# Attention maxima cut into parts of 512 keys, two shared banks for maxima and rows, and loads issued when the scores end

## The chip, the cores and the metric

The kernel runs on one core of a Trainium2 chip. The metric is the device time of one execution in microseconds; a kernel's time is the median of its runs.

## What is computed

Three layers run over 1024 tokens of width 1024 (the second and the third also see 256 context tokens). The change lies in the attentions of layers two and three:

```python
def gqa_attend(q, k, v):          # 16 query heads, 4 key heads, width 64
    s = jnp.einsum('bqhgd,bkhd->bhgqk', q, k).astype(jnp.float32) * (GQA_HEAD_DIM ** -0.5)
    p = jax.nn.softmax(s, axis=-1).astype(v.dtype)
    return jnp.einsum('bhgqk,bkhd->bqhgd', p, v)

def mla_attend(q_nope, q_rope, k_nope, k_rope, v):   # 16 heads, width 64 + 32
    s = (jnp.einsum('bqhd,bkhd->bhqk', q_nope, k_nope)
         + jnp.einsum('bqhr,bkr->bhqk', q_rope, k_rope)).astype(jnp.float32) * ((MLA_NOPE + MLA_ROPE) ** -0.5)
    p = jax.nn.softmax(s, axis=-1).astype(v.dtype)
    return jnp.einsum('bhqk,bkhd->bqhd', p, v)
```

Both take 1280 keys (256 of them context). In gqa the 256 context queries are attended as well, over the context keys alone.

## The kernel before

Float32 products are made of high and low parts. The class `Attention` (L1779) is used twice: `gqa` (three chunks of queries c: 512, 512 and the 256 context queries) and `mla` (two chunks of 512). A Fori loop runs over 8 pairs of heads; within a pair the steps k are unrolled (`self.steps`), one step being one tile of 128 keys against one chunk of queries: 22 steps a head in gqa (10, 10 and 2), 20 in mla.

In a step TensorE makes the scores (`scores`, L1964: two matmuls in gqa, three in mla, into one of two banks `self.S`), ScalarE takes exp and then the high part (`probs`, L2024), GpSimd, or VectorE in steps 3 and 8 of each ten, the low part (`low`, L2058), and TensorE three matmuls of `values` (L1984) that lag by `LAG` = 3 steps. At the end of a chunk ScalarE makes 1/denominator (`rden`, L2036: Ln, then Exp) and VectorE multiplies by it and by the gate (`final`, L2095), both in the step in which that chunk's last values are made.

The softmax needs the row maxima before the scores. They are made from the high parts of the queries: `maxima` (L1939) makes the scores of 128 queries against all 1280 keys, in three matmuls into the three banks of `PMX`, and one VectorE reduction (L2083) takes their maximum. After the tiles of a chunk `diag` (L2086) spreads the maxima over a diagonal, `bcast` (L1956) turns that into rows with a matmul by ones into the bank `self.BC`, and ScalarE's `row` (L2017) copies the one row that is needed into the query tile, where it enters the score matmul. Which step of a head makes which maxima, for the other chunks or for the next head, stands in the list `plan` (L1826 to L1832), four tiles for a chunk of 512 and two for the context chunk. All engines follow their own instructions in order: in a step, TensorE does the planned tasks, then scores, then the lagging values; VectorE does the reductions and the diagonal, then the low part of the step before, then `final`.

SyncE (`sp`, L1905) waits until all values of a head are made, then loads keys, values and queries of the head after the next into its buffers. The first maxima of a head wait for all of these (`loaded`).

## Time and profile before

| | us |
|---|---|
| median of 3 runs | 3587.86 |
| lowest and highest of them | 3587.32, 3591.61 |
| profiled execution | 3586.85 |
| its span, first to last instruction | 3585.0 |
| TensorE busy in the span | 3351.6 |
| mean granted TensorE clock, as a share | 0.977 |

The gqa stage lies at about 1819 to 2385 us of the span, the mla stage at about 2917 to 3490 us. A timeline row gives start, duration, engine and operation, and in brackets how long the engine had been idle and what ended that. A row of groups gives the busy time and the mean of one instruction, then the idle time ahead of the group.

### The profile page before, as it was taken

Reading aid. Unit: us, or ns where it says so; the run is one execution under the profiler, and the core shown is the slowest. Engines: PE = TensorE matmul, PEld = TensorE weight load, DVE = VectorE, ACT = ScalarE, POOL = GpSimd, SP = SyncE. Lnnn points to the kernel's source line nnn. Section 1 sums busy time; section 2 is a strip of 40 time slices with the busy share of each in tenths; the row PEclk is TensorE's granted clock in tenths of the full one; section 3 lists DMA queues with packets and bytes.
Section 4 is the critical chain, followed back from the end, with each engine's and each line's share of the span. In section 5 each row is a group of like instructions: output and inputs, shape, how many; then the busy total and the mean of one; then the engine's idle time right before and its main releaser. Section 6 shows DMA issues by size and latency. Waiting matters only on the chain.

```text
span 3585.0 us, 47856 instructions
## 1 busy us (share of the span) xinstructions
PE 3351.6 (93%) x14934; PEld 2655.1 (74%) x14934; DVE 2186.5 (61%) x2655; ACT 1793.4 (50%) x3060; POOL 1535.2 (43%) x977
## 2 busy tenths in 40 slices
PE   7999999999999999799889999989888989999999
PEld 5777877778888887587777777767765667777767
DVE  6674877477575757447246666666558865555551
ACT  3343868242010101434158888861465657887870
POOL 3303444434444444510156666656210026666652
PEclk9999999999999999899999999999999989999999
DMA  2134232311212121123433443412254344332311
GB/s 99 53 117 119 75 77 81 119 41 66 75 59 88 55 86 35 58 102 115 124 89 66 102 85 76 103 64 89 97 197 149 118 118 111 65 82 53 76 42 71
DMA packets 196086, 313.52 MB, mean 87 GB/s; under 512 B 100928, under 2 KB 111680, under 8 KB 195968
## 3 DMA queue, kind: packets, MB, share of 16 engines
q1 hardware_dynamic: 195968, 312.01, 29.8%
q8 instruction: 67, 1.10, 0.1%
q14 instruction: 51, 0.42, 0.0%
HBM read 234.02 MB, written 77.92 MB: 87 GB/s over the span
## 4 chain that ended last, share of the span: by engine, by line
PE 68%; DVE 12%; issue 7%; ACT 6%; POOL 3%; DMA 2%; SPq 2%; DVEq 0%; ACTq 0%; POOLq 0%
PE PBX L281 10%; PE PBX L283 10%; PE PBX L282 10%; PE PMX L281 5%; PE PMX L282 5%; PE PMX L283 5%; PE PMX L1952 4%; PE PD L1993 2%; PE PD L1994 2%; PE PD L1995 2%; PE PD L856 2%; DVE gqa_m L2083 1%; PE PBX L1977 1%; PE PBX L1976 1%; PE PBX L1978 1%
## 5 line engine op out<-in xcount | busy, mean ns | idle before, releaser
L216 POOL TENSOR_TENSOR w_hi<-w_stage,zero 128x1024 fp32r<-128x1024 f32 (+2 forms) x123 | 229.1, 1863 | 1263.4 <-PE PBX L283 789.3
L2061 POOL TENSOR_TENSOR gqa_pl<-gqa_pf,gqa_ph 128x512 fp32r<-128x512 f32 (+1 forms) x288 | 370.9, 1305 | 186.3 <-ACT gqa_ph L2034 185.7
L2061 POOL TENSOR_TENSOR mla_pl<-mla_pf,mla_ph 128x512 fp32r<-128x512 f32 x256 | 351.8, 1383 | 206.9 <-ACT mla_ph L2034 202.7
L2083 DVE TENSOR_REDUCE gqa_m<-PMX 128x1 f32<-128x1280 f32 (+1 forms) x158 | 200.9, 1271 | 173.6 <-PE PMX L1952 172.7
L218 POOL TENSOR_TENSOR w_lo<-w_stage,w_hi 128x1024 fp32r<-128x1024 f32 (+2 forms) x123 | 299.9, 2438 | 9.7
L1678 ACT ACTIVATE conv_in<-PBX 128x512 f32<-128x512 f32 x66 | 39.6, 601 | 480.6 <-PE PBX L283 476.6
L2083 DVE TENSOR_REDUCE mla_m<-PMX 128x1 f32<-128x1280 f32 x126 | 187.3, 1487 | 89.5 <-PE PMX L1952 88.9
L2029 ACT ACTIVATE mla_pf<-PBX 128x512 f32<-128x512 f32 x320 | 190.1, 594 | 98.0 <-PE PBX L1978 88.1
L2029 ACT ACTIVATE gqa_pf<-PBX 128x512 f32<-128x512 f32 (+1 forms) x352 | 202.1, 574 | 52.8 <-PE PBX L1981 48.6
L2034 ACT ACTIVATE gqa_ph<-gqa_pf 128x512 fp32r<-128x512 f32 (+1 forms) x352 | 215.6, 612 | 13.8
L281 PE MATMUL PBX<-ffn_hi,w_hi 128*128 128x512 f32 x528 | 207.5, 393 | 8.5 <-DVE ffn_lo L653 8.5
L2034 ACT ACTIVATE mla_ph<-mla_pf 128x512 fp32r<-128x512 f32 x320 | 202.2, 632 | 13.2 <-ACT mla_pf L2029 0.8
L283 PE MATMUL PBX<-ffn_hi,w_lo 128*128 128x512 f32 x528 | 206.2, 391 | 0.0
L282 PE MATMUL PBX<-ffn_lo,w_hi 128*128 128x512 f32 x528 | 206.2, 390 | 0.0
L1705 DVE SCALAR_TENSOR_TENSOR conv_out<-conv_in,VEC,conv_out 128x1024 f32<-128x1024 f32 x88 | 187.0, 2125 | 12.8 <-DVE conv_out L1701 0.6
L281 PE MATMUL PBX<-l_hi,w_hi 128*128 128x512 f32 (+1 forms) x408 | 161.8, 397 | 22.6 <-DVE l_lo L653 17.5
L1701 DVE TENSOR_SCALAR conv_out<-conv_in,VEC 128x1024 f32<-128x1024 f32 x44 | 73.8, 1678 | 137.6 <-ACT conv_in L1678 137.4
L432 DVE SCALAR_TENSOR_TENSOR PMX<-mod_w,cond_s 128x1024 f32<-128x1024 f32 x96 | 151.7, 1581 | 5.7 <-DVE PMX L432 0.8
L1440 POOL TENSOR_TENSOR swa_pl<-swa_pf,swa_ph 128x512 fp32r<-128x512 f32 x64 | 81.2, 1269 | 158.2 <-ACT swa_ph L1384 158.0
L283 PE MATMUL PBX<-l_hi,w_lo 128*128 128x512 f32 (+1 forms) x408 | 148.9, 365 | 0.0
L282 PE MATMUL PBX<-l_lo,w_hi 128*128 128x512 f32 (+1 forms) x408 | 148.5, 364 | 0.0
L281 PE MATMUL PBX<-h_hi,w_hi 128*128 128x512 f32 x336 | 138.5, 412 | 7.8 <-POOL w_lo L1426 5.7
(411 smaller groups left out, 9915.1 us busy)
## 6 DMA issues: line engine op xcount, KB each, us to landing
mod_w<-in_w_mod SPq DMA_DIRECT2D x48, 512.0 KB, 3.5
w_stage<-in_w_up SPq DMA_DIRECT2D x44, 512.0 KB, 3.4
w_stage<-in_w_go SPq DMA_DIRECT2D x24, 512.0 KB, 3.8
gqa_k<-kh_d SPq DMA_DIRECT2D x32, 320.0 KB, 4.9
gqa_q<-qh_d SPq DMA_DIRECT2D x32, 320.0 KB, 7.7
w_stage<-in_w_down SPq DMA_DIRECT2D x24, 384.0 KB, 3.0
qh_d<-heads_qh SPq DMA_DIRECT2D x32, 256.0 KB, 2.0
ql_d<-heads_ql SPq DMA_DIRECT2D x32, 256.0 KB, 2.3
```

The lines of the kernel that those rows point to most:

```text
L216: pool.tensor_tensor(w_hi[s][:, 0:st.cols], w_stage[s][:, 0:st.cols], z, ALU.add).then_inc(w_hi_done, 1)
L218: pool.tensor_tensor(w_lo[s][:, 0:st.cols], w_stage[s][:, 0:st.cols], w_hi[s][:, 0:st.cols].bitcast(F32), ALU.subtract).then_inc(w_split, 1)
L281: pe.matmul(ps, wh, xh, start=first, stop=False)
L282: pe.matmul(ps, wh, xl, start=False, stop=False)
L283: return pe.matmul(ps, wl, xh, start=False, stop=last)
L432: dve.scalar_tensor_tensor(out=PMX[:, C:3 * C], in0=bufs[s], scalar=1.0, in1=conds[j], op0=ALU.mult, op1=ALU.mult, accum_out=MOD[:, bass.d ...
L1705: dve.scalar_tensor_tensor(out=y, in0=CU[s][:, j:j + S], scalar=w(j), in1=y, op0=ALU.mult, op1=ALU.add).then_inc(conv_step, 1)
L1952: mm = pe.matmul(MX[:, s - lo_:e - lo_], self.Q[q][0][0:mr, o:o + P], self.K[q][0][0:mr, s:e], start=True, stop=True)
L2029: act.activation(self.PF[k % 4][:, 0:n], self.S[k % 2][:, 0:n], ACT.Exp, scale=self.scale)\
L2034: act.activation(self.PH[k % 4][:, 0:n], self.PF[k % 4][:, 0:n], ACT.Copy).then_inc(self.hi, 1)
L2061: eng.tensor_tensor(self.PL[k % 4][:, 0:n], self.PF[k % 4][:, 0:n], self.PH[k % 4][:, 0:n].bitcast(F32), ALU.subtract).then_inc(self.lo_dv ...
L2083: dve.tensor_reduce(self.M[g % 2][:, t:t + 1], MX[:, 0:w], AX.X, ALU.max, negate=True)\
```

## The change

- Maxima are made and reduced in parts of 512, 512 and 256 keys, each with a matmul, a wait and a reduction of its own (a unit). Units alternate between two banks, `self.MX`; a unit waits until the reduction before the last has ended. A small extra reduction takes the maximum over the parts (`NEG`) ahead of the diagonal.
- The rows go through the same two banks, as units, and VectorE copies them (`row`), in place of ScalarE. Units and rows are planned anew: a tile takes two steps, part 0 in the first and parts 1 and 2 in the second; in gqa the maxima of chunk 1 lie in steps 0 to 5 and its row in step 7, those of the context in 7 and 8 (row 10), those of the next head in 10 to 17 (row 19), and its chunk 1's first tile in 19 and 20. In mla: 0 to 5 (row 7), 9 to 16 (row 18), 18 and 19.
- The freed banks go to scores (three in gqa, four in mla) and, in gqa, to a third output bank. The ring of probabilities has 6 buffers in gqa and 5 in mla, in place of 4. Values lag by 4 steps, in place of 3; `final` runs 2 steps after that on VectorE and writes through the mix tile.
- The two key tiles of the context chunk become one step of 2 x 256 columns (21 steps a head in gqa).
- Loads: high keys and queries are issued when the last scores of the buffer's head have ended, and have a semaphore of their own that the maxima wait for; low queries and values come later, when the values have ended, for head 1 behind the gate's load.

```diff
-        CR_PV2, CR_SC, CR_B, CR_E, CR_ROW2, CR_R, CR_N, CR_FIN2 = 4, 1, 2, 2, 1, 1, 2, 1
+        CR_SC, CR_N, CR_FIN2 = 1, 3, 1
...
-            LAG = 3
+            LAG = 4
...
+                self.PF = [scope.sb(f"{name}_pf{b}", [P, C]) for b in range(ring)]
+                self.PH = [scope.sb(f"{name}_ph{b}", [P, C], R32) for b in range(ring)]
+                self.PL = [scope.sb(f"{name}_pl{b}", [P, C], R32) for b in range(ring)]
+                self.M = scope.sb(f"{name}_m", [P, 4, 3])
+                self.NEG = scope.sb(f"{name}_neg", [P, 4])
+                self.D = scope.sb(f"{name}_d", [P, 4, P], R32)
...
-                self.S = [PB[0], PB[1]]
-                self.BC = PB[2]
-                self.O = [PD[0], PD[1]]
+                self.S = [PB[0], PB[1], PB[2]] + [PMX[:, 2 * C:3 * C]] * self.mla
+                self.NS, self.NP = len(self.S), len(self.PF)
+                self.O = [PD[0], PD[1], PMX[:, 2 * C:3 * C]][:len(chunks)]
+                self.MX = [PMX[:, 0:C], PMX[:, C:2 * C]]
+
+
+                self.groups = [[(t,) for t in keys[c]] if len(keys[c]) > 2 else [tuple(keys[c])]
+                               for c in range(len(chunks))]
+                self.steps = [(q, c, g, x == 0, x == len(self.groups[c]) - 1) for q in range(2)
+                              for c in range(len(chunks)) for x, g in enumerate(self.groups[c])]
...
+                def tiles(at, first, count, step):
+                    return [(step + 2 * t + min(p, 1), "max", at, first + t, p) for t in range(count) for p in range(3)]
 
                 if self.mla:
-                    plan = [(2 * t, "max", (0, 1), t) for t in range(4)] + [(8, "bcast", (0, 1), 0)]
-                    plan += [(10 + 2 * t, "max", (1, 0), t) for t in range(4)] + [(18, "bcast", (1, 0), 0)]
+                    plan = tiles((0, 1), 1, 3, 0) + [(7, "row", (0, 1), 0, 0)]
+                    plan += tiles((1, 0), 0, 4, 9) + [(18, "row", (1, 0), 0, 0)]
+                    plan += tiles((1, 1), 0, 1, 18)
                 else:
-                    plan = [(2 * t, "max", (0, 1), t) for t in range(4)] + [(8, "bcast", (0, 1), 0)]
-                    plan += [(8 + 2 * t, "max", (0, 2), t) for t in range(2)] + [(12, "bcast", (0, 2), 0)]
-                    plan += [(12 + 2 * t, "max", (1, 0), t) for t in range(4)] + [(21, "bcast", (1, 0), 0)]
+                    plan = tiles((0, 1), 1, 3, 0) + [(7, "row", (0, 1), 0, 0)]
+                    plan += [(7 + t, "max", (0, 2), t, 0) for t in range(2)] + [(10, "row", (0, 2), 0, 0)]
+                    plan += tiles((1, 0), 0, 4, 10) + [(19, "row", (1, 0), 0, 0)]
...
+                parts = [(K[0][0:64, :], kh, self.loaded_max)]
+                parts += [(K[1][0:64, :], kl, self.loaded)] if self.mla else \
+                         [(K[0][64:128, :], kl, self.loaded_max), (K[1][0:64, :], kh, self.loaded)]
+                for to, src, done in parts:
+                    sp.dma_start(to.bitcast(F32), src).then_inc(done[q], 16)
...
+                for lo in ((0,) if self.mla else (0, 64)):
+                    sp.dma_start(self.Q[q][0][lo:lo + r, :].bitcast(F32), qh_d[bass.ds(h * r, r), 0:self.nq])\
+                      .then_inc(self.loaded_max[q], 16)
...
-                    sp.wait_ge(self.pv, i * self.SB + CR_PV2)
-                    self.load_kv(sp, 1, kv_row(i, 1))
+                    sp.wait_ge(self.scores, i * self.SB + CR_SC)
+                    self.load_k(sp, 1, kv_row(i, 1))
                     self.load_q(sp, 1, i * 2 + 1)
+                    sp.wait_ge(self.pv, i * self.SB + self.NP)
 
                     sp.wait_ge(self.fin, i * (2 * self.NC) + CR_FIN2)
                     sp.dma_start(self.G[:, :], gate_d[bass.ds(i, 1), :, 0:self.nq].rearrange("o p n -> (o p) n"))\
                       .then_inc(self.gate_loaded, 16)
+                    self.load_q_lo(sp, 1, i * 2 + 1)
+                    self.load_v(sp, 1, kv_row(i, 1))
                     if not last:
-                        sp.wait_ge(self.pv, i * self.SB + (CR_PV2 + self.SB // 2))
-                        self.load_kv(sp, 0, kv_row(i + 1, 0))
+                        sp.wait_ge(self.scores, i * self.SB + (CR_SC + self.SB // 2))
+                        self.load_k(sp, 0, kv_row(i + 1, 0))
                         self.load_q(sp, 0, i * 2 + 2)
+                        sp.wait_ge(self.pv, i * self.SB + (self.NP + self.SB // 2))
+                        self.load_q_lo(sp, 0, i * 2 + 2)
+                        self.load_v(sp, 0, kv_row(i + 1, 0))
...
-                def maxima(i, q, c, t, tile, first_of_head, head, MX=PMX, free=CR_R):
-                    if first_of_head and q == 1:
+                def maxima(i, q, c, t, part, unit, new_head, head, MX=self.MX):
+                    if new_head and q == 1:
                         pe.wait_ge(self.const[1], self.const_n)
-                    if first_of_head:
-
-                        pe.wait_ge(self.loaded[q], head * self.load_inc + self.load_inc)
+                    if unit >= len(MX):
+
+                        pe.wait_ge(self.red, i * (2 * self.NU) + (unit - len(MX) + 1))
...
-                    lo_, hi_ = kt[0] * P, (kt[-1] + 1) * P
-                    for s in range(lo_, hi_, C):
-                        e = min(s + C, hi_)
-                        mm = pe.matmul(MX[:, s - lo_:e - lo_], self.Q[q][0][0:mr, o:o + P], self.K[q][0][0:mr, s:e],
-                                       start=True, stop=True)
-                    mm.then_inc(self.max, 1)
+                    lo, hi = self.part_keys(c, part)
+                    pe.matmul(MX[unit % len(MX)][:, 0:hi - lo], self.Q[q][0][0:mr, o:o + P], self.K[q][0][0:mr, lo:hi],
+                              start=True, stop=True).then_inc(self.max, 1)
...
+                    pe.wait_ge(self.red, i * (2 * self.NU) + (unit - len(self.MX) + 1))
+                    pe.matmul(self.MX[unit % len(self.MX)][:, 0:n], ones[:, :], self.D[:, 0:n // P, :], start=True, stop=True)\
+                      .then_inc(self.max, 1)
...
+                        pe.wait_ge(self.red, i * (2 * self.NU) + (self.row_unit(q, c) + 1))
+                    if first and c == 0:
+
+                        pe.wait_ge(self.loaded[q], i * self.load_inc + self.load_inc)
+
+                    pe.wait_ge(self.exp, i * SB + (k + 1))
...
+                    for p in range(3):
+                        maxima(0, 0, 0, t, p, 3 * t + p, t == 0 and p == 0, 0, self.MX + self.S)
+                bcast(0, 0, 0, 12)
+                for p in range(3):
+                    maxima(0, 0, 1, 0, p, 13 + p, False, 0)
...
-                    act.activation(dst, self.BC[r:r + 1, 0:n], ACT.Copy).then_inc(self.row_done, 1)
...
+                    dve.tensor_reduce(self.M[:, t, part:part + 1], MX[unit % len(MX)][:, 0:hi - lo], AX.X, ALU.max)                       .then_inc(self.red, 1)
+
+                def diag(i, c, g, unit):
+                    m = self.chunks[c][1] // P
+                    parts = 1 if len(self.keys[c]) == 2 else 3
+                    dve.wait_ge(self.red, i * R + (unit + 1))
+                    dve.tensor_reduce(self.NEG[:, 0:m], self.M[:, 0:m, 0:parts], AX.X, ALU.max, negate=True)\
+                       .then_inc(self.neg, 1)
+                    dve.wait_ge(self.neg, i * (2 * NC) + (g + 1))
+                    dve.tensor_tensor(self.D[:, 0:m, :], ident_f[:, :].unsqueeze(1).to_broadcast([P, m, P]),
+                                      self.NEG[:, 0:m].unsqueeze(2).to_broadcast([P, m, P]), ALU.mult)\
+                       .then_inc(self.diag, 1)
+
+                def row(i, q, c, unit):
+                    o, n = self.chunks[c]
+                    r = self.row
+                    dve.wait_ge(self.max, i * R + (unit + 1))
+                    dve.tensor_copy(self.Q[q][0 if self.mla else 1][r:r + 1, o:o + n], self.MX[unit % 2][r:r + 1, 0:n])\
                        .then_inc(self.red, 1)
...
-                    dve.tensor_tensor(self.T[h, 0:n], self.O[x % 2][0:64, 0:n], self.RD[:, 0:n], ALU.mult)\
+                    m = self.mix[h, bass.ds(i, 1), o:o + n].rearrange("p o n -> p (o n)")
+                    dve.tensor_tensor(m, self.O[c][0:64, 0:n], self.RD[64 * (x % 2):64 * (x % 2) + 64, 0:n], ALU.mult)\
...
+                row(0, 0, 0, 12)
+                for p in range(3):
+                    maxima(0, 1, 0, p, 1, 13 + p)
...
-                self.run(dve, step, lambda i, k: final(i, k) if self.steps[k][4] else None)
+                self.run(dve, step, lambda i, k: final(i, k) if self.steps[k][4] else None, lag=self.LAG + 2)
```

## Rows read from the trace of the kernel before

**Rows 1.** Stretches (us): PE, PEld, DVE, ACT, POOL busy (x count), granted clock, DMA share, GB/s.

```profile
1960.00:2100.00 140.00, 128.36 (x569) 99.87 (x568) 86.38 (x94) 122.13 (x216) 95.63 (x75) 1.00 0.41 84
3060.00:3200.00 140.00, 137.76 (x595) 108.21 (x594) 79.83 (x75) 112.76 (x189) 88.70 (x65) 1.00 0.31 67
```

**Rows 2.** By tile: score matmuls: ns min/median/max, first and last start; shapes.

```profile
L1980 PE MATMUL PBX<-gqa_q,gqa_k x352: 277/395/628, 1828.8 to 2375.7; 128*128 128x512 f32 x160, 128*128 128x256 f32 x16
...
L1976 PE MATMUL PBX<-mla_q,mla_k x320: 391/396/632, 2928.2 to 3481.0; 97*128 97x512 f32 x160
```

**Rows 3.** Timeline, gqa, PE: start us, duration, engine, line, output<-inputs.

```profile
2037.18 0.28 PE L1994 MATMUL PD<-gqa_ph,gqa_v 128*128 128x256 f32 x1
...
2037.30 0.28 PE L1995 MATMUL PD<-gqa_pl,gqa_v 128*128 128x256 f32 x1
...
2042.53 0.39 PE L1980 MATMUL PBX<-gqa_q,gqa_k 128*128 128x512 f32 x1
...
2044.87 0.73 PE L1952 MATMUL PMX<-gqa_k,gqa_q 128*128 128x512 f32 x3
```

**Rows 4.** TensorE waits in 1829:2375 (gqa), then 2928.3:3481 (mla): us, times, longest.

```profile
PE PMX L1952 <- DVE gqa_m L2083: 30.3, 31, 1.1
PE PBX L1980 <- ACT gqa_pf L2029: 6.9, 16, 0.8
PE PBX L1961 <- DVE gqa_d L2091: 3.6, 13, 0.3
PE PMX L1952 <- DMA gqa_q<-qh_d: 3.0, 7, 0.8
...
PE PMX L1952 <- DVE mla_m L2083: 7.8, 28, 0.4
PE PMX L1952 <- DMA mla_q<-ql_d: 2.2, 2, 1.9
```

**Rows 5.** Timeline, gqa: one stall; [idle before <-what ended it].

```profile
2038.75 0.68 DVE L2102 TENSOR_TENSOR gqa_t<-PD,gqa_rd 64x512 f32<-64x512 f32 x1 [1.64 <-ACT gqa_rd L2046]
...
2039.58 0.69 DVE L2107 TENSOR_TENSOR MIX<-gqa_t,gqa_gate 64x512 f32 x1
...
2040.29 1.49 DVE L2083 TENSOR_REDUCE gqa_m<-PMX 128x1 f32<-128x1280 f32 x1
...
2041.84 0.85 PE L1952 MATMUL PMX<-gqa_k,gqa_q 128*128 128x512 f32 x3 [1.03 <-DVE gqa_m L2083]
```

**Rows 6.** Groups by form, gqa stage: busy us, mean ns | idle before.

```profile
L2083 DVE TENSOR_REDUCE gqa_m<-PMX 128x1 f32<-128x1280 f32 x126 | 187.3, 1487 | 162.2 <-PE PMX L1952 161.3
...
L2061 DVE TENSOR_TENSOR gqa_pl<-gqa_pf,gqa_ph 128x512 fp32r<-128x512 f32 x64 | 53.1, 830 | 28.7 <-ACT gqa_ph L2034 28.3
...
L2091 DVE TENSOR_TENSOR gqa_d<-ident_f,gqa_m 128x512 fp32r<-128x512 f32 x32 | 25.7, 802 | 3.0
...
L2102 DVE TENSOR_TENSOR gqa_t<-PD,gqa_rd 64x512 f32<-64x512 f32 x32 | 21.9, 683 | 58.9 <-ACT gqa_rd L2046 58.9
...
L2046 ACT ACTIVATE gqa_rd<-gqa_rd 64x512 f32<-64x512 f32 x32 | 20.2, 632 | 1.0
```

**Rows 7.** Timeline, gqa: exps of ScalarE, a maxima matmul with its reduction.

```profile
2042.09 0.60 ACT L2029 ACTIVATE gqa_pf<-PBX 128x512 f32<-128x512 f32 x1
...
2043.27 0.60 ACT L2029 ACTIVATE gqa_pf<-PBX 128x512 f32<-128x512 f32 x1
...
2048.60 0.29 PE L1952 MATMUL PMX<-gqa_k,gqa_q 128*128 128x256 f32 x1
...
2048.93 0.42 DVE L2083 TENSOR_REDUCE gqa_m<-PMX 128x1 f32<-128x256 f32 x1 [0.72 <-PE PMX L1952]
```

**Rows 8.** Timeline, start of the gqa stage.

```profile
1819.60 0.82 PE L1952 MATMUL PMX<-gqa_k,gqa_q 128*128 128x512 f32 x3 [2.82 <-DVEq L2076]
...
1827.97 0.59 ACT L2022 ACTIVATE gqa_q<-PBX 1x512 fp32r<-1x512 f32 x1 [7.49 <-PE PBX L1961]
...
1828.80 0.63 PE L1980 MATMUL PBX<-gqa_q,gqa_k 128*128 128x512 f32 x1
```

More of the change, by code:

```diff
@@ L1779, in mixed_program, with __init__ @@
         class Attention:
-            LAG = 3
-            def __init__(self, name, scope, chunks, keys, scale, layout, mix, first):
+            LAG = 4
+            def __init__(self, name, scope, chunks, keys, scale, layout, mix, first, ring):
                 self.name, self.chunks, self.keys, self.scale, self.mix = name, chunks, keys, scale, mix
@@ L1964, in scores @@
                 def scores(i, k):
-                    q, c, t, first, _ = self.steps[k]
+                    q, c, tiles, first, _ = self.steps[k]
                     o, n = self.chunks[c]
                     if first:
-                        pe.wait_ge(self.row_done, i * (2 * NC) + (q * NC + c + CR_ROW2 + 1))
-                    pe.wait_ge(self.exp, i * SB + (k - 2 + CR_E + 1))
-                    s = self.S[k % 2][:, 0:n]
-                    keys = slice(t * P, (t + 1) * P)
+                        pe.wait_ge(self.red, i * (2 * self.NU) + (self.row_unit(q, c) + 1))
@@ L1982, in scores @@
                     mm.then_inc(self.scores, 1)
                 def values(i, k):
-                    q, c, t, first, last_ = self.steps[k]
+                    q, c, tiles, first, last_ = self.steps[k]
                     n = self.chunks[c][1]
@@ L2750, in mixed_program @@
         tmp = Scope()
[L2751 removed]
+        mla = Attention("mla", tmp, CHUNKS_X, (range(NT), range(NT)), 96 ** -0.5, "mla", MIX1, mla_first, 5)
         tmp.close()
```

211 lines of the change are left out of this document (94 added, 117 removed).

## Prediction, made before the changed kernel was run

> **What bounds the kernel now.** The stretches come first [rows 1]: in a steady 140 us TensorE is busy for 128.36 us in gqa and 137.76 in mla, the clock granted in full, with ScalarE next in both (122.13 and 112.76). But a matmul's 0.39 us of busy time overlaps its neighbour's, so I count starts instead. Ten matmuls of 512 columns start in 2.34 us, 0.234 each, and a 256-column one takes 0.12 [rows 3]. A pair of heads has, in gqa, 236 matmuls of 512 columns and 42 of 256 (per head: scores 40 and 4, values 60 and 6, maxima 16 and 10, rows 2 and 1): 55.2 + 5.0 = 60.3 us of bare stream. In mla it has 276 and 16: 66.5 us. From the first to the last score matmul the gqa stage runs 546.9 us and mla 552.8 [rows 2], so 68.4 and 69.1 us a pair. TensorE loses 8.1 us a pair in gqa and 2.6 in mla: 65 and 21 us over the 8 pairs. That is all this change can win by ordering.
>
> The waits say who holds it [rows 4]: the maxima matmuls wait for VectorE's reductions (31 times, 30.3 us, and 28 times, 7.8 us), then come exp (6.9 us), the diagonal (3.6) and loads (3.0 and 2.2). Each stop costs some 0.1 us more than its wait: the three maxima matmuls after one last 0.85 us, in a stream 0.73 [rows 3, 5]. The timeline of one stop shows the mechanism [rows 5]: VectorE, idle for 1.64 us until 1/denominator is there, does the two multiplications of `final`, only then the 1.49 us reduction, and TensorE resumes 0.06 us after that.
>
> **The change, part by part.**
>
> *Reductions.* 1487 ns for 1280 columns and 423 for 256 [rows 6, 7] give 1.04 ns a column and a fixed 157 ns, so 0.69 us for 512. A tile in parts costs 2 x 0.69 + 0.42 = 1.80 in place of 1.49: 16 tiles a pair, 5.0 us more. Small reductions over the parts: 6 x 0.17 = 1.0. Rows on VectorE: no row of its own; its multiplication of 512 PSUM elements took 0.683 [rows 6], so 0.69 x 4 + 0.42 x 2 = 3.6 (bounds: half of that, and 0.83 each as for `low`). VectorE has now 16 x 1.49 + 4 x 0.42 + 8 x 0.83 (`low`) + 4.1 (diagonals, 0.80 and half of that) + 7.1 (`final`, 1.37 and 0.84) = 43.3 us a pair in gqa, and will have 52.9 of some 66. Nothing of this is on TensorE's path by itself; it is where TensorE meets it.
>
> The Trainium skill, "VectorE: DVE Perf Modes", section on the TRN2 errata, speaks against small parts: its 120 + FD cycles for PSUM sources would make a tile 0.25 us dearer, and it advises at least 512 elements a tile, which the third part has not. By it the added work would be 4.0 instead of 5.0 us a pair. The rows' 0.31 us are close to that.
>
> *Two banks.* A reduction starts 0.33 us after its 256-column matmul, which lasts 0.29 [rows 7]; for 512 columns (0.39) I take 0.42. In gqa a step is 5 x 0.234 = 1.17 us plus its units. Part 0 at 0 is reduced by 1.11; part 2, which needs that bank, comes at 1.40 + 0.23 = 1.63: slack 0.46. Part 1 at 1.40 is reduced by 2.51; the next tile's part 0 comes at 2.92: slack 0.35. So an undisturbed tile costs no wait (before, the slack was 0.6 with a single handshake a tile). A mla step is 1.40: slack 0.7 and 0.6.
>
> *`final` two steps later.* VectorE's idle wait for 1/denominator (58.9 us in gqa [rows 6]) goes; its 0.68 + 0.15 + 0.69 = 1.5 us [rows 5] remain, and I follow them in gqa, head by head. `final` of the last head's chunk 1 now falls in step 4, behind `low`. From the start of step 4: part 0 is reduced by 1.11; `low` of step 3 needs ScalarE, which made 1/denominator (0.60 + 0.63 [rows 6]) before the exp of step 3, so it starts at about 1.84 and ends at 2.67; `final` ends at 4.1; parts 1 and 2 of step 5 at 5.0, the small reduction 5.3, the diagonal (0.80) 6.2. TensorE reaches the row's matmul in step 7 after 1.40 + 1.52 + 1.17 = 4.1 us and stands for 2.2, 2.3 with the restart; the scores of step 7 and the values of step 3 queue behind it, and ScalarE and GpSimd wait for those. The second meeting is in steps 15 to 17: `final` of chunk 0 (3.0 to 4.5 us after step 14) pushes part 0 of step 16 to 5.1, and part 2 of step 17, due at 4.55, waits 0.65 + 0.1. Together 3.1 a head, 6.2 a pair; the rest of the head keeps its slack. Against 8.1 that wins 1.9, and 15 us over 8 pairs.
>
> *The same in mla.* There `final` falls in step 5 behind the diagonal, a step is 0.23 us longer, and the diagonal is done at about 4.2 us where step 7 comes at 4.8. Of the 2.6 us I leave 0.7 for loop turns and a late diagonal: 1.9 a pair, 15 us.
>
> *Score banks, ring, lag, context step.* Three and four banks take off the waits for exp [rows 4]. ScalarE's own pace is 1.18 us a step (0.60 exp, then the high part, next exp 1.18 later [rows 7]). 42 steps make 49.6 us a pair, with 1/denominator some 7: 57 of 66. It loses the row copies and 2 steps' worth of context tiles and is no bound. The lag of 4 adds a step to low parts' time. No gain counted beyond the waits, which are in the 8.1 and 2.6.
>
> *Loads.* They must beat step 9 or 10 instead of 12 or 10, but start when scores end, and three transfers fewer stand among them (low queries and values go behind). They cost at most the 5.2 us of waits seen [rows 4], which are in the sums; a new wait for the late loads would have to outlast a whole head (33 us). On SyncE the loads for head 1 now stand behind the wait for `final` of the last pair, some 7 us into the head: covered by 25 us.
>
> *Start of each stage.* Before: first maxima at 1819.60, row copy 1827.97, first scores 1828.80 [rows 8]. After, 12 reductions in place of 4 add 4 x 0.16 (back to back they overlap), the small one 0.2, and three more units stand ahead of the first scores, the third waiting for a reduction of the second bank's user: 0.8. 1.6 us a stage, 3 in all. Bounds 0 and 6.
>
> **The sum.** 3586.85 (the profiled execution; 1.0 under the median of 3587.86, 1.85 over its span, which stands for what lies around it and stays) - 15 - 15 + 3 = 3559.9. On the median's scale 3560.
>
> **The rivals.**
>
> *A: the meeting at step 7 does not happen* (ScalarE and VectorE catch up, or `low` is not late). For: the slips are worked out from means, and TensorE's other short waits let them catch up. Against: `final` lies there by construction, with 1.5 us. Without it 16 x 2.1 = 34 us more: 3526.
>
> *B: VectorE becomes the bound of gqa.* The diagonal, of the size of a part, takes 0.80 on average, and `low` 0.83, where 0.69 is their bare length. If parts of 512 take 0.95, 32 x 0.26 = 8.3 us come to 52.9, and its waits in order for ScalarE and TensorE some 4: 65 to 68 us a pair. gqa then wins 0 to 10, mla its 15: about 3578. Against: 126 reductions of 1280 columns average 1487, and one in the timeline took 1.49 [rows 5, 6]: nothing stretches them, though GpSimd works beside them. The Trainium skill, "SBUF — State Buffer", section on who interferes with whom, says that a reduction never contends with GpSimd while a two-input operation from SBUF does; by it this rival is unlikely. The rows agree, as far as 1280 columns go.
>
> *C: slower.* As B, and each of the 52 reductions of a pair also pays the 0.14 us or so that a waiting VectorE instruction shows ahead of it (0.15 between the multiplications of `final` [rows 5]): 52 x 0.14 = 7.3, so 72 us a pair in gqa. It decides from 68.4. gqa +25, mla 0, starts +3: 3615.
>
> *D: it doesn't do what it says.* Waits in the loops may go from one to the other semaphore without anything moving: if gqa's order is set by ScalarE's lag, only mla's part comes: 3575. This one goes with B.
>
> **How the numbers follow.** Forecast as summed (3540 to 3572) 0.5; A and what lies between 0.17; B and D (3572 to 3588) 0.2; C and beyond 0.13. Predicted 3560. The range must leave out no more than 0.2: from 3520 (A, with its start at no cost) to 3592. A measurement of this kernel tells about 0.2%, 7 us, from no change. Faster, under 3580.7: 0.5 + 0.17 + 0.11 = 0.78; within, 0.11; slower, over 3595.0: 0.11.
>
> **What would show it.** Waits of TensorE: those for reductions in gqa should fall from 30.3 to under 12 us, those for the diagonal rise from 3.6 to about 30, in 16 large pieces of some 2 us; in mla both stay under 4. Waits for exp gone. Per pair, the first to last scores should give 66.5 and 67.2 us. A part of 512 reduced in 0.69 us, a row copied on VectorE in 0.5 to 0.7. B or C would show parts of 0.8 and more and many short waits of maxima matmuls. The forecast is wrong if the large waits for the diagonal are missing (A), if ScalarE shows no idle time between steps in gqa, or if the first scores of a stage start over 4 us later than before.

## The result and the profile after

| us | before | after |
|---|---|---|
| median | 3588.26 | 3612.78 |
| lowest to highest (4 runs each) | 3587.32 to 3591.61 | 3608.64 to 3618.45 |
| profiled execution | 3586.85 | 3611.21 |
| its span | 3585.0 | 3608.9 |
| gqa, first to last score matmul | 546.9 | 546.9 |
| mla, first to last score matmul | 552.8 | 568.9 |

The changed kernel is slower: its time is 1.0068 of the time before [1.0053, 1.0083]. 3560 was forecast, with 3592 as the upper end. The head of the page after:

```profile
span 3608.9 us, 49183 instructions
...
PE 3354.7 (93%) x14934; PEld 2673.7 (74%) x14934; DVE 2352.2 (65%) x3327; ACT 1751.6 (49%) x2948; POOL 1527.1 (42%) x961
```

The stages, by tile, answer to [rows 2]. Line, operation, count, ns min/median/max, first and last start, shapes:

```profile
L2016 PE MATMUL PBX<-gqa_q,gqa_k x352: 280/395/629, 1833.2 to 2380.1; 128*128 128x512 f32 x160, 128*128 128x256 f32 x16
...
L2012 PE MATMUL PBX<-mla_q,mla_k x240: 391/396/628, 2936.1 to 3503.6; 97*128 97x512 f32 x120
L2012 PE MATMUL PMX<-mla_q,mla_k x80: 392/400/632, 2943.4 to 3505.0; 97*128 97x512 f32 x80
```

So gqa takes 546.9 us as before and mla 568.9 (2936.1 to 3505.0), 16.1 more. Of the span's 23.9 us the rest is 2.3 at the start of each stage, and 2.1 before the gqa stage and 1.2 between the stages, where the code is the same: the first maxima of gqa started between 1818.8 and 1822.1 us in the traces of this study.

TensorE's waits over the stages, after, answer to [rows 4]: us in total, times, longest. The first three lines are gqa, the last two mla:

```profile
PE PMX L1993 <- DVE gqa_d L2116: 28.1, 16, 1.9
PE PMX L1986 <- DVE gqa_m L2107: 21.1, 16, 1.8
PE PMX L1986 <- DVE gqa_q L2124: 3.9, 13, 0.4
...
PE PMX L1993 <- DVE mla_d L2116: 23.7, 15, 1.7
PE PMX L1986 <- DVE mla_m L2107: 1.3, 1, 1.3
```

The waits for exp and for loads are gone. In mla a new one stands: once a head a row's matmul (L1993) waits 1.6 us for the diagonal. It is the row of step 18, for the next head. Where that comes from is read on VectorE, in the groups by form of the mla stage (busy us, mean ns of one | idle before):

```profile
L2107 DVE TENSOR_REDUCE mla_m<-PMX 128x1 f32<-128x512 f32 x246 | 170.0, 691 | 160.9 <-PE PMX L1986 157.1
...
L2116 DVE TENSOR_TENSOR mla_d<-ident_f,mla_neg 128x512 fp32r<-128x512 f32 x31 | 37.2, 1200 | 1.1
L2138 DVE TENSOR_TENSOR MIX<-MIX,mla_gate 64x512 f32 x28 | 37.2, 1328 | 1.6
L2124 DVE CAST mla_q<-PMX 1x512 fp32r<-1x512 f32 x31 | 21.6, 697 | 11.1 <-PE PMX L1993 10.6
L2134 DVE TENSOR_TENSOR MIX<-PD,mla_rd 64x512 f32 x28 | 19.1, 681 | 0.7
```

The parts and the row copies cost what was forecast. The gate multiplication (L2138) takes 1.33 us and the diagonal 1.20, against 0.69 bare [rows 5] and 0.80 on average [rows 6]. The timeline of steps 15 to 18 of one head in mla, VectorE, then GpSimd, then TensorE (start, us, operation, [idle before <- what ended it]):

```profile
3035.25 0.67 DVE L2134 TENSOR_TENSOR MIX<-PD,mla_rd 64x512 f32 x1
3036.05 1.70 DVE L2138 TENSOR_TENSOR MIX<-MIX,mla_gate 64x512 f32 x1
3037.68 1.00 DVE L2107 TENSOR_REDUCE mla_m<-PMX 128x1 f32<-128x512 f32 x2
3038.72 0.17 DVE L2113 TENSOR_REDUCE mla_neg<-mla_m 128x4 f32<-128x12 f32 x1
3038.92 1.77 DVE L2116 TENSOR_TENSOR mla_d<-ident_f,mla_neg 128x512 fp32r<-128x512 f32 x1
...
3035.92 1.28 POOL L2086 TENSOR_TENSOR mla_pl<-mla_pf,mla_ph 128x512 fp32r<-128x512 f32 x1 [2.92 <-ACT mla_ph L2066]
3037.16 1.74 POOL L2086 TENSOR_TENSOR mla_pl<-mla_pf,mla_ph 128x512 fp32r<-128x512 f32 x1
...
3038.78 0.40 PE L2032 MATMUL PD<-mla_pl,mla_v 128*128 128x512 f32 x1
3040.81 0.49 PE L1993 MATMUL PMX<-mla_d,ones 128*128 128x512 f32 x1 [1.63 <-DVE mla_d L2116]
```

GpSimd begins a low part at 3035.92. The gate multiplication, which reads two operands from SBUF, comes 0.13 us later, and ends 0.55 us after GpSimd's has ended (3037.20), as if it had waited for that end. The diagonal, again two operands from SBUF, meets the low part that follows (2950 ns for two, from 3038.87) and takes 1.77. The multiplication between them by 1/denominator, with one operand from PSUM, stays at 0.67, and so do the reductions. Two meetings of 1.0 us put the diagonal 2 us later, and TensorE stands for 1.63.

This one head is no exception. Of the 31 gate multiplications of 512 columns inside the mla stage after, 29 began while a GpSimd operation was at work, and each ended 0.54 to 0.55 us after that operation; so did 16 of the 31 diagonals. The other 2 and the other 15 took 0.69. The pattern stands in the trace of before as well, in 13 of 31 diagonals of gqa (VectorE, then GpSimd, whose operation ends at 2047.66, 0.55 before the diagonal's end):

```profile
2047.27 0.94 DVE L2091 TENSOR_TENSOR gqa_d<-ident_f,gqa_m 128x512 fp32r<-128x512 f32 x1
...
2046.37 1.29 POOL L2061 TENSOR_TENSOR gqa_pl<-gqa_pf,gqa_ph 128x512 fp32r<-128x512 f32 x1
```

The head's other row, that of step 7, waits for nothing. There `final` stands behind the diagonal:

```profile
3019.48 0.69 DVE L2116 TENSOR_TENSOR mla_d<-ident_f,mla_neg 128x512 fp32r<-128x512 f32 x1
...
3020.93 0.39 PE L1993 MATMUL PMX<-mla_d,ones 128*128 128x512 f32 x1
```

Then something follows that the forecast had not in it. TensorE 1.7 us after that stop, and two stretches of the windows view (start:end, length, busy us (x count) of PE, PEld, DVE, ACT, POOL, granted clock, DMA share, GB/s):

```profile
3042.55 0.63 PE L2032 MATMUL PD<-mla_pl,mla_v 128*128 128x512 f32 x1
...
3043.62 0.63 PE L2012 MATMUL PMX<-mla_q,mla_k 97*128 97x512 f32 x1
3044.05 0.63 PE L2013 MATMUL PMX<-mla_q,mla_k 96*128 96x512 f32 x1
...
3042.40:3045.90 3.50, 3.50 (x11) 2.78 (x10) 1.99 (x4) 1.83 (x4) 0.00 (x0) 0.52 0.00 0
3045.90:3076.00 30.10, 29.95 (x132) 24.05 (x130) 20.14 (x33) 24.30 (x41) 19.59 (x15) 1.00 0.34 70
```

For 3.4 us the matmuls start 0.43 apart and not 0.234: the granted clock is 1.2 GHz, then 2.4 again. Such a stretch costs 1.7 us, as much as the wait ahead of it. There are 8 in mla after, none in mla before; 3 in gqa after, 2 before. (Every stage in every trace also begins with a long one, 13.7 to 23.9 us, which starts ahead of its first scores and is not counted.) mla then adds up: 530 of bare stream (what the runs below show once no wait is left; the forecast had 8 x 66.5 = 532) + 23.7 of waits + 15 x 0.16 (a stop lets the matmul ahead of it run out its 0.39 instead of 0.234) + 8 x 1.7 = 569.7, and 568.9 was measured.

### The profile page after: what moved, and what is told of

The parts are those of the page before. It is cut to its first block, busy times and chain, and to the rows that moved or that the text cites. A ratio compares the mean times of both kernels' runs of the same rounds, so it can differ in the third digit from the quotient of the medians.

```text
span 3608.9 us, 49183 instructions
## 1 busy us (share of the span) xinstructions
PE 3354.7 (93%) x14934; PEld 2673.7 (74%) x14934; DVE 2352.2 (65%) x3327; ACT 1751.6 (49%) x2948; POOL 1527.1 (42%) x961
## 4 chain that ended last, share of the span: by engine, by line
PE 70%; DVE 11%; issue 8%; ACT 5%; POOL 3%; DMA 0%; DVEq 0%; SPq 0%; ACTq 0%; POOLq 0%
PE PBX L281 10%; PE PBX L283 10%; PE PBX L282 10%; PE PMX L281 5%; PE PMX L282 5%; PE PMX L283 5%; PE PMX L1986 3%; PE PD L2030 3%; PE PD L2031 3%; PE PD L2032 3%; PE PD L856 2%; PE PBX L2013 1%; PE PBX L2014 1%; PE PBX L2012 1%; PE PBX L2017 1%
## 5 line engine op out<-in xcount | busy, mean ns | idle before, releaser
L2086 POOL TENSOR_TENSOR gqa_pl<-gqa_pf,gqa_ph 128x512 fp32r<-128x512 f32 x272 | 364.6, 1351 | 197.0 <-ACT gqa_ph L2066 191.7
L2107 DVE TENSOR_REDUCE mla_m<-PMX 128x1 f32<-128x512 f32 x378 | 215.8, 599 | 166.6 <-PE PMX L1986 162.7
L2107 DVE TENSOR_REDUCE gqa_m<-PMX 128x1 f32<-128x512 f32 (+1 forms) x410 | 227.8, 584 | 138.8 <-PE PMX L1986 135.2
L2061 ACT ACTIVATE gqa_pf<-PBX 128x512 f32<-128x512 f32 x336 | 199.5, 594 | 92.8 <-PE PBX L2017 85.4
L2066 ACT ACTIVATE gqa_ph<-gqa_pf 128x512 fp32r<-128x512 f32 x336 | 212.4, 632 | 13.2
L2061 ACT ACTIVATE mla_pf<-PBX 128x512 f32<-128x512 f32 x240 | 142.8, 595 | 107.8 <-PE PBX L2014 102.5
L1986 PE MATMUL PMX<-gqa_k,gqa_q 128*128 128x512 f32 (+1 forms) x410 | 135.0, 371 | 28.6 <-DVE gqa_m L2107 21.4
```

The costliest lines, as they stand in the source:

```text
L1986: pe.matmul(MX[unit % len(MX)][:, 0:hi - lo], self.Q[q][0][0:mr, o:o + P], self.K[q][0][0:mr, lo:hi], start=True, stop=True).then_inc(self ...
L2061: act.activation(self.PF[k % self.NP][:, :], self.S[k % self.NS][:, :], ACT.Exp, scale=self.scale)\
L2066: act.activation(self.PH[k % self.NP][:, :], self.PF[k % self.NP][:, :], ACT.Copy).then_inc(self.hi, 1)
L2086: eng.tensor_tensor(self.PL[k % self.NP][:, :], self.PF[k % self.NP][:, :], self.PH[k % self.NP][:, :].bitcast(F32), ALU.subtract).then_in ...
L2107: dve.tensor_reduce(self.M[:, t, part:part + 1], MX[unit % len(MX)][:, 0:hi - lo], AX.X, ALU.max) .then_inc(self.red, 1)
```

## The experiments

All are edits of the changed kernel. "(one)" marks a single run, for which no interval can be given. "gqa" and "mla" are the us from first to last score matmul; the times before beside them had medians of 3587 to 3588.

| run | median us | ratio to before | gqa | mla |
|---|---|---|---|---|
| after | 3612.78 | 1.0068 [1.0053, 1.0083] | 546.9 | 568.9 |
| e1 GpSimd's low parts short | 3568.67 (one) | | 541.3 | 530.0 |
| e2 rows later | 3573.16 | 0.9958 [0.9942, 0.9975] | 537.1 | 542.0 |
| e3 every long row's wait filled | 3639.41 | 1.0138 [1.0121, 1.0155] | 566.3 | 579.4 |
| e7 filled only where it waited | 3594.87 | 1.0022 [1.0013, 1.0032] | 544.7 | 557.1 |
| e5 `final` later | 3597.09 | 1.0025 [1.0016, 1.0035] | 553.2 | 547.5 |
| e8 e2 and `final` at 7 | 3604.99 | 1.0050 [1.0033, 1.0067] | 566.9 | 544.1 |
| e6 e2 and e5 | 3589.63 | 1.0009 [1.0000, 1.0019] | 554.9 | 544.1 |
| e9 loads later again | 3615.51 (one) | | 550.6 | 569.7 |
| e10 e1 and e2 | 3541.09 (one) | | 514.5 | 529.7 |
| e12 gate on GpSimd | 3573.54 | 0.9958 [0.9941, 0.9974] | 540.7 | 532.9 |
| e11 e2 and e12 | 3558.09 | 0.9920 [0.9904, 0.9937] | 530.4 | 529.1 |

The theory: VectorE's operations with two SBUF operands wait for GpSimd's, which makes the diagonal late, and the stop that follows costs its length and often a half-clock stretch. The rivals: the loads that now start when a head's scores end; VectorE's sheer amount of work on two banks; the row's place in the order alone.

### e1: GpSimd's operations made short

The low parts that GpSimd makes are cut to 64 of 512 columns; the rest of those tiles stays zero, so this part of the computation is left out.

```
-  self.low(pool, i, k)
+  pool.wait_ge(self.hi, i * self.SB + (k + 1))
+  ...
+  pool.tensor_tensor(self.PL[b][:, 0:64], self.PF[b][:, 0:64],
+                     self.PH[b][:, 0:64].bitcast(F32), ALU.subtract).then_inc(self.lo_pool, 1)
```

> The changed kernel with GpSimd's low parts made over 64 of 512 columns (the low parts of the other columns are left out and stand at zero); all else, VectorE's order too, stays. Theory (VectorE's multiplications with two SBUF inputs wait for GpSimd's operations, and TensorE then waits for the diagonal): every gate multiplication and every diagonal of 512 takes 0.69 us in place of 1.2 to 1.3 on average; TensorE's waits for the diagonal in mla fall from 23.7 us to under 4 and the half-clock stretches inside mla vanish, so first to last scores of mla go from 568.9 to about 535 us; in gqa from 546.9 to about 530. Rival (VectorE simply has too much to do for two banks): its load is unchanged, and mla stays within 5 us of 568.9.

mla fell by 38.9 us to 530.0. Its groups, mla, and its TensorE row over 470 us of the stage:

```profile
L2119 DVE TENSOR_TENSOR mla_d<-ident_f,mla_neg 128x512 fp32r<-128x512 f32 x31 | 21.5, 692 | 1.1
L2141 DVE TENSOR_TENSOR MIX<-MIX,mla_gate 64x512 f32 x28 | 20.4, 730 | 1.6
...
2960.00:3430.00 470.00, 470.00 (x2065) 382.06 (x2064) 312.08 (x541) 377.92 (x624) 79.50 (x226) 1.00 0.35 79
```

The diagonal is back to 0.69 us and the gate multiplication to 0.73; in these 470 us TensorE is never idle and the clock never falls. The order of the work and the number of VectorE's operations are the same as in after, so neither by itself makes mla slower. In gqa only 5.6 us were won, where some 17 had been expected: the waits for reductions fell from 21.1 to 7.5, but the stop for the diagonal stayed,

```profile
PE PMX L1993 <- DVE gqa_d L2119: 28.7, 15, 2.1
PE PMX L1986 <- DVE gqa_m L2110: 7.5, 16, 1.8
```

and 13 half-clock stretches (22 us) followed such stops, where after had 3. That stop is thus the one that the forecast had worked out from the order, not from contention. The timeline of after agrees: all of VectorE's operations ahead of the stop have their bare lengths.

```profile
2188.50 0.69 DVE L2138 TENSOR_TENSOR MIX<-MIX,gqa_gate 64x512 f32 x1
...
2190.47 0.69 DVE L2116 TENSOR_TENSOR gqa_d<-ident_f,gqa_neg 128x512 fp32r<-128x512 f32 x1
...
2191.30 0.49 PE L1993 MATMUL PMX<-gqa_d,ones 128*128 128x512 f32 x1 [1.92 <-DVE gqa_d L2116]
```

### e2: the rows one step later

The row of the next chunk goes from step 7 to 8, that of the next head from 18 to 19 (gqa: 19 to 20), between parts of a tile (the mla plan; gqa's likewise, its context tiles at 7 and 8):

```
-  plan = tiles((0, 1), 1, 3, 0) + [(7, "row", (0, 1), 0, 0)]
-  plan += tiles((1, 0), 0, 4, 9) + [(18, "row", (1, 0), 0, 0)]
-  plan += tiles((1, 1), 0, 1, 18)
+  plan = tiles((0, 1), 1, 3, 0) + [(8, "row", (0, 1), 0, 0)]
+  plan += tiles((1, 0), 0, 4, 9)
+  plan += [(18, "max", (1, 1), 0, 0), (18, "max", (1, 1), 0, 1),
+           (19, "row", (1, 0), 0, 0), (19, "max", (1, 1), 0, 2)]
```

> The changed kernel with the rows of 512 one step later (7 to 8; 18 to 19 in mla, 19 to 20 in gqa), behind the first parts of the next tile. Theory: the diagonal is 1.6 us late in mla and a step is 1.40 us, so the wait shrinks to 0.2 us and with it the half-clock stretches go: mla 568.9 to about 536 us, gqa 546.9 to about 530, total about 3560. Rival (two banks with three handshakes a tile hold TensorE up): a late row changes nothing, total 3605 to 3618.

Faster than before by 0.42%. No stop for the diagonal is left, and the granted clock is 1.00 over 1850 to 2350 and 2960 to 3430 us, though the diagonal takes as long as in after (0.92 and 1.21 us): it is only waited for no more. The direction was as expected, the size was not reached: gqa came to 537.1 for 530 expected, mla to 542.0 for 536, the total to 3573 for 3560. mla kept 12 us over its bare stream. The waits, gqa, then mla:

```profile
PE PMX L1985 <- DVE gqa_m L2106: 47.8, 46, 1.8
...
PE PMX L1992 <- DVE mla_m L2106: 4.7, 14, 0.4
```

In gqa the time now stands as 46 waits of some 1.0 us for reductions: VectorE is behind and TensorE meets it at the next part. In mla the list shows 0.34 a head, but by the starts of the matmuls more is lost: at 3060.37 the row starts 0.52 us behind its place in the stream, and at 3026.7 the next two matmuls behind such a row start 0.36 and 0.10 behind theirs, so about 1 us a head.

### e3 and e7: the wait filled with matmuls

Six matmuls into the bank that the row will overwrite stand ahead of the wait for the diagonal; in e3 at each row of 512, in e7 only at the row that waited in after. For them the wait for that bank's reduction had to move ahead as well.

```
 def bcast(i, c, g, unit, q=0):
+    pe.wait_ge(self.red, i * (2 * self.NU) + (unit - len(self.MX) + 1))
+    if n == C:                             # e7: if c == (0 if self.mla else 1)
+        for _ in range(6):
+            pe.matmul(self.MX[unit % len(self.MX)][:, 0:n], ones[0:mr, :], self.K[q][0][0:mr, 0:C],
+                      start=True, stop=True)
     pe.wait_ge(self.diag, i * (2 * NC) + (g + 1))
-    pe.wait_ge(self.red, i * (2 * self.NU) + (unit - len(self.MX) + 1))
```

> The changed kernel with six matmuls of 512 columns, whose result is overwritten, ahead of each row matmul of 512, inside TensorE's wait for the diagonal (1.4 of some 1.7 us). Theory (a wait that long takes the clock to half for 3.4 us afterwards, which costs 1.7 us each): the waits' ends stay where they were, the half-clock stretches inside mla (8 at least) vanish, mla loses 13 us, total about 3596. Rival (the clock stretches are incidental, the idle time itself is all): total stays at 3608 to 3618, or grows.

> The changed kernel with six matmuls of 512 columns, whose result is overwritten, ahead of only those row matmuls at which TensorE stands for 1.6 to 1.8 us (chunk 0's row in mla, chunk 1's in gqa); the run before this one put them at every row of 512 and so paid 16 x 1.4 us twice where TensorE had nothing to wait for. Theory (each such wait is followed by 3.4 us at half clock, 1.7 us lost, 8 times in mla and 3 times in gqa): mla's first to last scores 568.5 - 13.7 = 555 us, gqa's 546.6 - 5 = 541, total about 3594. Rival (the idle time alone costs, the clock nothing): both stages as in the changed kernel, or longer by what the matmuls overrun, total 3608 to 3620.

e3 missed by 43 us, and the cause was in its edit: six matmuls are 1.4 us at each of two rows a head, 22.5 us a stage at the row that had not waited. With both rows: 530 + 45 + 3.1 (waits left) = 578.1 in mla; 579.4 was measured. e7 came out near what was expected in mla, 557.1 for 555, against 568.9 in after, and 530 + 22.5 + 3.1 = 555.6 is the same sum. In gqa it gave back 2.2 of the 6 us expected: the wait for the reduction, now ahead of the six matmuls, takes 0.53 us, and with their 1.4 that is more than the 1.76 of after. The same stretch of mla, after, then e7:

```profile
2945.00:3480.00 535.00, 511.30 (x2174) 411.16 (x2173) 363.05 (x565) 397.05 (x655) 329.16 (x239) 0.97 0.31 70
...
2945.00:3480.00 535.00, 531.93 (x2315) 428.42 (x2314) 368.70 (x573) 407.85 (x671) 338.09 (x245) 1.00 0.31 70
```

The row comes as late in the head as in after, but TensorE works meanwhile, the clock stays at 2.4 GHz throughout, and 11.8 us come back. That is the price of the half-clock stretches, put at 8 x 1.7 = 13.6, separated from that of the waits. e3 has no such stretch either, in both stages.

### e5, e8 and e6: `final` moved

`final` falls one step later in mla and two in gqa (e5); one step later in both, with e2's rows (e8); as in e5, with e2's rows (e6).

```
-  self.run(dve, step, ..., lag=self.LAG + 2)
+  self.run(dve, step, ..., lag=self.LAG + (3 if self.mla else 4))    # e5, e6
+  self.run(dve, step, ..., lag=self.LAG + 3)                         # e8
```

> The changed kernel with VectorE's final multiplications one step later in mla (7 behind the scores' step) and two in gqa (8), so that they stand behind the diagonals and not before them; rows stay at 7 and 18 or 19. Theory: the diagonal no longer waits for a multiplication that itself waits for GpSimd; TensorE's waits for diagonals in mla fall from 23.7 to under 6 us, in gqa from 28 to under 6, waits for reductions in gqa from 21 to under 8; mla about 536, gqa about 505 us, total about 3540. Rival (VectorE's load, two banks): the same work in another order gives at most 5 us.

> The changed kernel with rows one step later and the final multiplications one step later too (7 behind the scores' step) in both stages: they then stand behind the diagonals. Theory (placement, collision with GpSimd, clock): in mla both waits of the changed kernel are gone, 535 us against 541.6 with late rows alone; in gqa the waits for part reductions behind the final multiplications in steps 5 and 17 (47.5 us with late rows alone) fall under 25, 515 us against 536.8; total about 3545, faster than the kernel before by 1%. Rival (VectorE's load on two banks holds gqa): gqa stays at 537 or above, total 3566 or above.

> As the previous one, but in gqa the final multiplications two steps later (8). Theory: they fall in steps 17, 6 and 7, the last beside the context tiles and near the low part of a GpSimd-busy stretch; with late rows the row copy no longer stands behind them, so the 552.8 us of gqa with row 7 and the same lag fall to about 520; mla 535; total about 3550. Rival (load of VectorE): gqa stays at 550.

In mla all three go the right way: 547.5, 544.1 and 544.1 instead of 568.9, though 535 or 536 had been expected. In gqa all three missed: 553.2, 566.9 and 554.9, each worse than after, where 505, 515 and 520 had been expected. `final` left the diagonal's way and met others. In gqa, the low parts of VectorE in e5 (692 ns in after), the diagonal of the context chunk in e6, and the gate multiplication in e8:

```profile
L2086 DVE TENSOR_TENSOR gqa_pl<-gqa_pf,gqa_ph 128x512 fp32r<-128x512 f32 x63 | 56.0, 888 | 17.1 <-ACT gqa_ph L2066 16.7
...
L2115 DVE TENSOR_TENSOR gqa_d<-ident_f,gqa_neg 128x256 fp32r<-128x256 f32 x16 | 20.4, 1276 | 0.6
...
L2137 DVE TENSOR_TENSOR MIX<-MIX,gqa_gate 64x512 f32 x28 | 38.7, 1381 | 1.6
```

In after the last two took 0.95 and 1.22. e8's gqa also holds 9 half-clock stretches (15 us), with waits of up to 2.4 us; e5's and e6's hold none. This is no account of each stop: which operation meets which in these three was read only from such means, and it stays open whether a place exists at which none meet. What follows is that these times can't be had from the order by counting bare lengths, which is how all three were expected and how the forecast was made.

### e9: the loads moved back

High keys and queries are issued when the head's last values have ended, for one buffer as here, for the other likewise:

```
-  sp.wait_ge(self.scores, i * self.SB + CR_SC)
+  sp.wait_ge(self.pv, i * self.SB + self.NP)
```

> The changed kernel with its early loads put back: high keys and queries are issued when the head's last values have ended, as before, and not when its scores have. Theory: the maxima now start at step 9 or 10, so some of them wait for the queries again, up to 1 us each, at most 8 us in a stage; the large waits stay where they are. Rival (early loads disturb something and are the cause of the loss): mla comes back towards 553 us.

550.6 and 569.7 us: mla does not come back, so the early loads are not the cause of the loss. The waits for loads that were expected did not come either. gqa is 3.7 us longer, and it has 6 half-clock stretches where after had 3.

### e10: short GpSimd operations and rows later

Both edits, of e1 (with the same part of the low parts left out) and of e2.

> Rows one step later, and GpSimd's low parts made over 64 of 512 columns (the others are left out, at zero). Theory (late diagonals, collisions with GpSimd and half-clock stretches are all there is): mla stays at the 530 us of the run with short low parts alone, since nothing was left there; gqa, 541.0 with short low parts (28.7 us of waits for diagonals and 13 half-clock stretches, 22 us) and 536.8 with late rows (47.5 us of waits for reductions behind stretched multiplications), falls to about 500 us, bare stream 482. Rival (VectorE's load on two banks also costs): gqa stays above 525.

mla is at its bare stream, 529.7. gqa is at 514.5, 32 us under after and 34 over its own bare stream of some 480:

```profile
PE PMX L1985 <- DVE gqa_m L2106: 47.8, 46, 1.8
...
PE PMX L1985 <- DVE gqa_m L2109: 25.6, 46, 1.8
```

The first line is e2's, the second e10's, both gqa: with the contention all but gone, 25.6 of 47.8 us of waits for reductions stay. About 500 had been expected if contention were all, over 525 by the rival; 514.5 lies between. So VectorE's work costs gqa something at its bare lengths too, about as much as contention does at this order. It is not the bound of the stage, as rival B of the prediction would have it: over 1850 to 2340 us VectorE is busy for 371.7 of 490. In the head at 2187 to 2220 the waits stand right behind the multiplications of `final`, 0.33 to 0.54 us each; that the order bunches its work is a reading of that, not a test.

### e12 and e11: the gate multiplication on GpSimd

e12 moves only `final`'s gate multiplication from VectorE to GpSimd, which does it between its own low parts, so that these two can't meet; e11 has e2's rows as well. Nothing is left out in either.

```
   def gate(i, k):                          # in pool()
       ...
+      pool.drain()
+      pool.wait_ge(self.norm, i * (2 * self.NC) + (q * self.NC + c + CR_N + 1))
+      pool.wait_ge(self.gate_loaded, i * 16 + 16)
+      pool.tensor_tensor(m, m, self.G[h, o:o + n], ALU.mult).then_inc(self.fin, 1)
+      pool.drain()
+  self.run(pool, step, gate, lag=self.LAG + 2)
   ...                                      # in final(), VectorE
-  dve.tensor_tensor(m, m, self.G[h, o:o + n], ALU.mult).then_inc(self.fin, 1)
```

> The changed kernel with only the gate multiplication moved to GpSimd; rows stay at steps 7 and 18 or 19, loads and banks as changed. Theory: in mla the diagonal was 1.6 us late behind a gate multiplication of 1.70 us; with that gone it is in time even for row 18, and mla goes from 568.5 to about 532 us without the rows being moved; in gqa the diagonal of step 5, 1.76 us late behind both halves of the final multiplications, is 0.7 us less late: 546.6 to about 537; total about 3567. Rival (late rows were what helped mla in the combined version): mla stays above 555.

> Rows one step later, and the multiplication by the gate made by GpSimd, in its own order, in place of VectorE; nothing is left out. Theory: of VectorE's operations with two SBUF inputs the gate's, the most stretched (1.22 and 1.33 us on average), is gone, so its 0.7 to 1.7 us no longer stand ahead of reductions: waits for reductions in gqa fall from 47.5 to under 25 us, gqa 536.8 to about 515, mla 541.6 to about 536; GpSimd gets some 5 us a pair more and has 15 to spare; total about 3547. Rival (GpSimd's queue becomes the bound, its low parts arrive late): waits of the values for GpSimd's low parts appear, over 20 us, and the total is 3573 or more.

In mla e12 came out as expected: 532.9 with no wait for the diagonal. One of the two meetings is enough to be rid of there, where the row had been nearly in time. In gqa it came to 540.7 for 537, and not in the way expected: the waits for the diagonal, which were to get shorter, stayed at 28.0 us, and those for reductions fell from 21.1 to 2.9. With the gate multiplication gone, the diagonal comes 0.7 us sooner and now meets a low part (GpSimd, VectorE, TensorE):

```profile
2183.45 1.26 POOL L2086 TENSOR_TENSOR gqa_pl<-gqa_pf,gqa_ph 128x512 fp32r<-128x512 f32 x1 [3.45 <-ACT gqa_ph L2066]
...
2183.90 1.36 DVE L2127 TENSOR_TENSOR gqa_d<-ident_f,gqa_neg 128x512 fp32r<-128x512 f32 x1
...
2185.39 0.49 PE L1993 MATMUL PMX<-gqa_d,ones 128*128 128x512 f32 x1 [1.88 <-DVE gqa_d L2127]
```

It takes 1.36 where it took 0.69, and what was won is lost again. 8 half-clock stretches followed such stops, 5 more than in after. e11 takes e2's rows for gqa's stop and is the fastest complete kernel here, 3558.09 us, 0.992 of before [0.9904, 0.9937]. It misses the 3547 expected of it in gqa (530.4 for 515). Its waits there:

```profile
PE PD L2029 <- POOL gqa_pl L2085: 18.2, 15, 1.3
PE PMX L1992 <- DVE gqa_d L2126: 7.8, 16, 0.6
PE PMX L1985 <- DVE gqa_m L2117: 4.7, 10, 1.8
...
L2104 POOL TENSOR_TENSOR MIX<-MIX,gqa_gate 64x512 f32 x28 | 37.2, 1328 | 11.3 <-issue 11.3
```

The multiplication takes GpSimd 1.33 us, and a low part that queues behind it now holds TensorE 15 times for 1.2 us. These 18.2 us come near the 20 that its rival had named. Still, the 47.8 us of waits for reductions in e2 have become 4.7.

## Why the prediction was wrong

*VectorE's arithmetic.* A part of 512 in 0.69 us (0.689 and 0.691 measured), the small reduction in 0.17 (0.167), a row copied in 0.69 (0.689 to 0.697): right. A tile of 1280 in parts takes 2 x 0.69 + 0.41 = 1.79, 0.30 over the 1.49 of before. An estimate from the 120 + FD cycles that the Trainium skill gives for PSUM sources ("VectorE: DVE Perf Modes", section on the TRN2 errata) is 0.25. Two of its terms failed. `final` was taken at 1.5 us from one stop [rows 5], in which its gate multiplication took 0.69; it now takes 1.22 in gqa and 1.33 in mla. The diagonal was taken at its mean of 0.80 [rows 6] and takes 0.91 and 1.20. The group of the gate multiplication in mla, before:

```profile
L2107 DVE TENSOR_TENSOR MIX<-mla_t,mla_gate 64x512 f32 x28 | 19.2, 686 | 4.7 <-DVE mla_t L2102 1.7
```

At its old place, in the step in which the last values are made, it met no low part in mla; at the new one it does. The prediction moved the operation and kept the length that it had where it stood. That a diagonal of 0.80 and a low part of 0.83 stand over a bare 0.69 was seen, under rival B, and put down as a possible stretch of reductions, the one kind that showed none. The diagonals of gqa before were in fact of two kinds, 18 of 0.69 and 13 of 0.94 to 1.05, and the mean of 0.80 belongs to neither. The Trainium skill, "SBUF — State Buffer", section on who interferes with whom, says that a two-input VectorE operation from SBUF contends with GpSimd's reads and a reduction does not. The traces agree: 1.70 and 1.77 us against 0.69 for the one, 0.69 unchanged for the other. The prediction quoted this rule against B and did not ask what it does to the operations that the change itself moved.

*Two banks.* "An undisturbed tile costs no wait": right, in e1 and e10 mla shows none.

*gqa, step 7.* 2.2 us were forecast for the diagonal, 16 times, and 28.1 us in 16 waits came, 1.8 each. Right, and by the mechanism given, since `final` and the diagonal have their bare lengths there and e1 keeps the stop.

*gqa, steps 15 to 17.* 0.65 each were forecast, 10 us; the waits for reductions are 21.1 and those for the copied row 3.9. Mis-sized: e1, where `final` is not stretched, has 7.5.

*mla.* This step failed ("The same in mla"). It followed one of the two rows of a head, that of step 7, where `final` falls behind the diagonal of step 5, and put the diagonal 0.6 us early. That held: the row never waits, and the diagonal is 0.76 early (3020.17 to 3020.93). The other row, that of step 18, it put at nothing without following it. There `final` of chunk 0 falls in step 15, ahead of the diagonal of step 16; for gqa the prediction had followed this very place, steps 15 to 17. At bare lengths it would still have been in time, but by little: in e1 the diagonal ends 0.2 to 0.4 us ahead of TensorE. Two meetings of 1.0 us are far more than that. In place of no wait stand 23.7 us in 15 waits, and behind 8 of them a half-clock stretch. The waits of before that the change was to remove did go (7.8 to 1.3, loads to none).

*The restart.* 0.1 us a stop was taken from before's short stops. It is 0.16 for those, and 1.7 more where the clock falls afterwards: 13.6 us in mla, 5 in gqa. Such stretches were rare before (2 in gqa, each behind waits of 0.41 and 1.03 us within 2.5 us), where the longest wait for a reduction was 1.1 us.

*Exp waits, loads.* Right: the waits for exp are gone, and so are those for loads; e9, one run, shows no gain from their old place.

*Start of each stage.* 1.6 us forecast, 2.3 measured (first maxima to first scores 11.5 for 9.2 in gqa, 12.6 for 10.3 in mla); within the bounds given.

*The rivals.* The total was rival C's (3615), the mechanism was not: no part is stretched, and the loss is in mla, which C left at 0. That the figures meet is chance. B and C were also priced loosely: against 68.4 us a pair, B's 65 to 68 win 3 to 27 us in gqa and not 0 to 10, and C's 72 lose 29 and not 25. The largest part is mla's: -15 forecast, +16.1 measured, 31 of the 53 us. gqa makes 15 (-15 forecast, 0 measured): 11 + 4 of longer waits at steps 15 to 17 and 5 of half clock, less the 7 that step 7 came out under, are 13 of them. Starts (1.6 over the 3 forecast), the 2.1 ahead of gqa and 1.2 between the stages are 5. The median, 1.6 over the profiled execution, is the rest.

What e1 undid in mla and e7 separated is shown. That VectorE's operation waits for GpSimd's rests on e1, on e12 and on the ends 0.55 us after GpSimd's. Why the clock fell after 8 of mla's 15 stops and after 3 of gqa's 16 is open: stops of 1.63 to 1.69 us were followed by a fall in some cases and not in others.

## What to carry to other kernels

An operation's length belongs to its place: before moving one, ask what runs on the neighbouring engine there, and cost each VectorE operation with two SBUF operands from both sides, alone and after the end of a GpSimd operation in progress. A margin smaller than one such meeting is no margin. A schedule that repeats has to be followed at every place where the moved operation falls, in each stage: here the place that was not followed held the loss. In an otherwise full TensorE stream, one stop of 1.6 us can cost twice its length; waits of 1.0 us in the mean brought a half-clock stretch 2 times in before's gqa and never in e2's. Moving the waiting matmul one step later (e2) was worth 40 us in all.
